# A ring of weight slots in a one-core MoE kernel: twelve slots with a four-slot stash, or sixteen slots in two halves

## What is computed

```python
def expert_choice_moe(h, w_router, w1, w3, w2):
    aff = jax.nn.softmax(jnp.einsum('bsd,de->bse', h, w_router).astype(jnp.float32), axis=-1)
    cap = CAPACITY_FACTOR * S // N_EXPERTS          # 32 tokens for each expert
    gate, idx = lax.top_k(aff.swapaxes(1, 2), cap)
    xe = jax.vmap(lambda hb, ib: hb[ib])(h, idx)

    def expert(args):
        xt, w1e, w3e, w2e = args
        return (jax.nn.silu(xt @ w1e) * (xt @ w3e)) @ w2e
```

## Time and profile before

| | us |
|---|---|
| median of 3 executions | 1844.26 (1843.57 to 1846.16) |
| the profiled execution, timed | 1841.69 |
| its span, first to last instruction | 1839.8 |
| first matmul with expert weights | 595.0 |
| last slot of the last expert arrives | 1830.51 |

### The profile page before, as it was taken

The page is one execution under the profiler, slowest core; times in us unless marked ns, Lnnn a source line. Parts: engine busy times, 40 slices in busy tenths (PEclk is TensorE's granted clock), DMA queues, the critical chain, the costliest instruction groups (busy, mean ns, idle before and its releaser), DMA issues.

```text
span 1839.8 us, 24014 instructions
## 1 busy us (share of the span) xinstructions
PE 1345.1 (73%) x10570; PEld 825.3 (45%) x10570; DVE 272.9 (15%) x555; ACT 226.6 (12%) x531; POOL 42.3 (2%) x68
## 2 busy tenths in 40 slices
PE   6998999999987676666665765666575665757565
PEld 4577888888565234232331423233142332414232
DVE  1215100006952000000010000101000010100001
ACT  1333221012133010010000001000000100000010
POOL 0001000002020000000000000000000000000000
PEclk9999999999998887777777777777777777777777
DMA  9746354242445999999999999999999999999998
GB/s 353 298 160 251 143 224 169 106 183 68 186 189 220 421 436 424 431 434 436 435 427 437 425 429 433 439 428 434 432 430 427 435 437 425 438 428 435 430 432 343
DMA packets 48248, 649.02 MB, mean 353 GB/s; under 512 B 3832, under 2 KB 6336, under 8 KB 31056
## 3 DMA queue, kind: packets, MB, share of 16 engines
q1 hardware_dynamic: 45152, 643.90, 82.9%
q10 hardware_dynamic: 2848, 3.55, 0.6%
q0 software_dynamic: 208, 1.00, 0.1%
HBM read 647.38 MB, written 1.06 MB: 352 GB/s over the span
## 4 chain that ended last, share of the span: by engine, by line
DMA 59%; PE 11%; DVE 1%; issue 1%; ACT 0%; SPq 0%; DVEq 0%; PEldq 0%; ACTq 0%
DMA ring<-in_w 59%; PE ps L1220 11%; DVE arena L1099 0%; DVE small L1103 0%; ACT arena L683 0%; DVE arena L1168 0%; DVE arena L1128 0%; DVE arena L1170 0%; DVE xT L1212 0%; ACT L708 0%; DVE arena L1187 0%; ACT arena L690 0%; SPq L369 0%; DVE arena L1078 0%; ACT arena L711 0%
## 5 line engine op out<-in xcount | busy, mean ns | idle before, releaser
L1220 PE MATMUL ps<-ring,table 128*32 128x352 f32 x4032 | 435.9, 602 | 270.3 <-DMA ring<-in_w 270.2
L1220 PEld LDWEIGHTS ps<-ring,table 128*32 128x32 f32 x4032 | 154.3, 140 | 536.8 <-issue 339.9
L1220 PE MATMUL ps<-ring,arena 128*32 128x256 f32 (+1 forms) x2818 | 197.0, 437 | 150.0 <-DMA ring<-in_w 149.8
L1220 PEld LDWEIGHTS ps<-ring,arena 128*32 128x32 f32 (+1 forms) x2818 | 102.7, 125 | 246.5 <-issue 149.1
L1220 PE MATMUL ps<-hT,ring 128*128 128x256 f32 (+1 forms) x880 | 194.7, 382 | 3.0 <-PE ps L1220 1.4
L1220 PEld LDWEIGHTS ps<-hT,ring 128*128 128x128 f32 (+1 forms) x880 | 165.0, 189 | 30.9 <-issue 6.2
L1220 PE MATMUL ps<-arena,ring 128*128 128x256 f32 (+1 forms) x800 | 175.2, 379 | 1.9 <-ACT arena L632 1.4
L1220 PEld LDWEIGHTS ps<-arena,ring 128*128 128x128 f32 x800 | 151.4, 190 | 23.3 <-issue 2.9
L1220 PE MATMUL ps<-arena 32*128 32x256 f32 (+10 forms) x532 | 91.5, 383 | 29.2 <-DVE xT L1212 12.2
L1220 PEld LDWEIGHTS ps<-arena,hT 128*128 128x128 f32 x512 | 104.1, 315 | 9.1 <-issue 9.1
L1220 PE MATMUL ps<-arena,hT 128*128 (+1 forms) x512 | 106.3, 387 | 1.8 <-DVEq L1196 1.8
(11 more groups left out here) (225 smaller groups left out, 540.5 us busy)
## 6 DMA issues: line engine op xcount, KB each, us to landing
ring<-in_w SPq DMA_DIRECT2D x76, 5632.0 KB, 32.9
ring<-in_w SPq DMA_DIRECT2D x19, 2816.0 KB, 28.3
ring<-in_w SPq DMA_DIRECT2D x35, 1408.0 KB, 31.2
ring<-in_w_ff SPq DMA_DIRECT2D x8, 4096.0 KB, 13.9
ring<-in_w_ada SPq DMA_DIRECT2D x6, 4096.0 KB, 15.2
ring<-in_w_in SPq DMA_DIRECT2D x3, 4096.0 KB, 13.9
ring<-in_w_in SPq DMA_DIRECT2D x5, 2048.0 KB, 19.2
ring<-in_w_out SPq DMA_DIRECT2D x2, 4096.0 KB, 12.8
```

The costliest lines, as they stand in the source:

```text
L1220: return pe.matmul(o, w, x, start=first, stop=last)
```

## The change

`ring` and `arena` become one tensor, `big`, and the ring now has 16 places; places 12 to 15 are where `stash` lay. Since 24 is not a multiple of 16, slot q of expert e lies at place (q + 8 * odd) % 16, where odd is 1 for odd experts. Two experts in turn therefore need different addresses, and the loops of PE and SP now have a body of two experts: PE's loop runs 7 times over experts (1, 2), (3, 4) to (13, 14), and expert 15 is written out once behind it, as expert 0 is ahead of it. The loops of ScalarE, VectorE and GpSimd stay as they were.

Experts 1 to 14 are loaded in six transfers of four slots. Expert 0's w2 is loaded in 1, 1, 2, 4 slots (`FIRST_W2`), right behind its other slots and ahead of expert 1; expert 15's w2 in 4, 2, 1, 1 (`LAST_W2`), as before. There are 133 transfers of expert weights before and 103 after: 11 for expert 0 in both, then 10 + 14 x 8 before and 14 x 6 + 8 after. SP waits for slots 16 back, not 12.

```diff
-NSLOT = 12
+UNIT_SLOTS = 12
+NSLOT = 16
-PIECES = (4, 4, 4, 4, 4, 2, 1, 1)
+FIRST_W2 = (1, 1, 2, 4)
+LAST_W2 = (4, 2, 1, 1)
...
-        ring = sb("ring", NSLOT * SLOT)
-        arena = sb("arena", AR)
+        big = sb("big", UNIT_SLOTS * SLOT + AR)
+        ring = big[:, 0:NSLOT * SLOT]
+        arena = big[:, UNIT_SLOTS * SLOT:]
...
-            for q, n, done in ((0, 1, s["lead_in"]), (1, 1, s["lead_in"]), (2, 2, piece_in[0])):
-                sp.wait_ge(s["w_used"], q + n)
-                slots(1, q, n, done)
...
-            with sp.Fori(0, NE - 2) as e:
-                for i, (q, n) in enumerate(PIECE_AT):
-                    sp.wait_ge(s["w_used"], NCHUNK * e + q + n + 2 * NCHUNK - NSLOT)
-                    piece(e + 2, i)
+            slots(0, 15, 1, piece_in[3])
+            q = 2 * C
+            for i, n in enumerate(FIRST_W2):
+                sp.wait_ge(s["w_used"], q + n - NSLOT)
+                slots(0, q, n, piece_in[4 + i // 3])
+                q += n
+
+            def pieces(e, odd, count=6):
+                for i in range(count):
+                    sp.wait_ge(s["w_used"], NCHUNK * e + 4 * (i + 1) - NSLOT)
+                    slots(e, 4 * i, 4, piece_in[i], odd)
+
+            with sp.Fori(1, NE - 1, 2) as e:
+                pieces(e, 1)
+                pieces(e + 1, 0)
+            pieces(NE - 1, 1, 4)
+            q = 2 * C
+            for i, n in enumerate(LAST_W2):
+                sp.wait_ge(s["w_used"], NCHUNK * (NE - 1) + q + n - NSLOT)
+                slots(NE - 1, q, n, piece_in[4] if i == 0 else last_in[i - 1], 1)
+                q += n
...
-            expert(0, first=True)
-            with pe.Fori(1, NE) as e:
-                expert(e)
+            expert(0, 0, first=True)
+            with pe.Fori(1, NE - 1, 2) as e:
+                expert(e, 1)
+                expert(e + 1, 0)
+            expert(NE - 1, 1, last=True)
```

More of the change, by code:

```diff
@@ L59 @@
 NVEC = sum(n for _, n in VEC.values())
-PIECE_AT = [(sum(PIECES[:i]), n) for i, n in enumerate(PIECES)]
-PIECE_OF = {q: i for i, (q, n) in enumerate(PIECE_AT)}
-assert sum(PIECES) == NCHUNK and all(q % C + n <= C and q % NSLOT + n <= NSLOT for q, n in PIECE_AT)
 def bank_plan():
@@ L247, in build @@
         halfgb = small[:, 88:96]
-        stash = ar(0, 4 * SLOT)
         yacc = xT_[:, :].rearrange("p (st n) -> p st n", st=ST)
@@ L272, in build @@
         unit_in2 = sem("unit_in_gate_columns")
-        piece_in = [sem(f"piece_in{i}") for i in range(len(PIECES))]
+        piece_in = [sem(f"piece_in{i}") for i in range(6)]
+        last_in = [sem(f"last_in{i}") for i in range(3)]
         s = {name: sem(name) for name in """
@@ L280, in build @@
             sq1_set n1_set t1_set h_set relu_set x1_set sq2_set n3_set n2_set up_set sgb_set pe_link
-            qsq_set qk_set rs16_set v_set    csq_set diag_set cvar_set x2_set sq3_set first_in stash_in lead_in sqp_set
+            qsq_set qk_set rs16_set v_set    csq_set diag_set cvar_set x2_set sq3_set first_in stash_in sqp_set
             lge_set wr2_set std_set rst_set lgs_set hnat_set yinit_set xe_set ye_set xe_full sc_full pgT_set hid_full he_set sg_set
@@ L365, in _, with slots @@
                     T["w2_2"].rearrange("e (p r) n -> p e (r n)", r=FR)]
-            def slots(e, q, n, done):
-                at, mat = q % NSLOT, q // C
+            def slots(e, q, n, done, odd=0):
+                at, mat = (q + 8 * odd) % NSLOT, q // C
                 sp.dma_start(ring[:, at * SLOT:(at + n) * SLOT],
                              mats[mat][:, e, (q - C * mat) * SLOT:(q - C * mat + n) * SLOT]).then_inc(done, 16)
-            def piece(e, i):
-                slots(e, *PIECE_AT[i], piece_in[i])
             sp.wait_ge(s["unit_used"], UNIT["qk"] + 1)
@@ L380, in _ @@
             sp.wait_ge(s["xr_set"], 1)
-            piece(0, 0)
+            slots(0, 0, 4, piece_in[0])
             slots(0, 4, 2, s["first_in"])
@@ L385, in _ @@
             slots(0, 8, 1, piece_in[2])
-            stashed = mats[1][:, 0, (12 - C) * SLOT:]
-            sp.dma_start(stash[:, 0:3 * SLOT], stashed[:, 0:3 * SLOT]).then_inc(s["stash_in"], 16)
+            slots(0, 12, 3, s["stash_in"])
             sp.wait_ge(s["std_set"], 1)
-            sp.dma_start(stash[:, 3 * SLOT:], stashed[:, 3 * SLOT:]).then_inc(piece_in[3], 16)
-            for q, n, done in ((0, 1, s["lead_in"]), (1, 1, s["lead_in"]), (2, 2, piece_in[0])):
-                sp.wait_ge(s["w_used"], q + n)
-                slots(1, q, n, done)
-            for i, (q, n) in enumerate(PIECE_AT):
[L394 to L400, removed]
-            with sp.Fori(0, NE - 2) as e:
-                for i, (q, n) in enumerate(PIECE_AT):
-                    sp.wait_ge(s["w_used"], NCHUNK * e + q + n + 2 * NCHUNK - NSLOT)
-                    piece(e + 2, i)
+            slots(0, 15, 1, piece_in[3])
[17 more added lines that the diff above has]
+                q += n
         @block.gpsimd
@@ L1756, in _, with expert @@
             pe.sem_inc(s["sc_full"], 1)
-            def expert(e, first=False):
+            FIRST_AT = ((0, piece_in[0], 1), (4, s["first_in"], 2), (6, piece_in[1], 1), (8, piece_in[2], 1),
+                        (12, s["stash_in"], 1), (15, piece_in[3], 1))
+            def expert(e, odd, first=False, last=False):
                 def gather(g):
@@ L1772, in expert @@
                         q = mat * C + c
-                        slot = q % NSLOT
+                        slot = (q + 8 * odd) % NSLOT
                         if mat == 0:
                             pe.wait_ge(s["xe_set"], C * e + c + 2)
-                        if q in PIECE_OF:
-                            pe.wait_ge(piece_in[PIECE_OF[q]], 16 * (e + 1))
-                        w = ring[:, slot * SLOT:(slot + 1) * SLOT]
[L1779 to L1785, removed]
+                        if first:
+                            for at, done, n in FIRST_AT:
+                                if q == at:
+                                    pe.wait_ge(done, 16 * n)
+                        elif c % 4 == 0:
+                            pe.wait_ge(piece_in[2 * mat + c // 4], 16 * e + 16)
+                        w = ring[:, slot * SLOT:(slot + 1) * SLOT]
                         for half in range(2):
@@ L1802, in expert @@
                 pe.wait_ge(s["pgT_set"], e + 1)
-                w2v = ring[:, 4 * SLOT:12 * SLOT].rearrange("p (r n) -> p r n", r=FR)
+                w2v = ring[:, 8 * odd * SLOT:8 * (odd + 1) * SLOT].rearrange("p (r n) -> p r n", r=FR)
+                steps = FIRST_W2 if first else LAST_W2 if last else (C,)
+                starts = [sum(steps[:i]) for i in range(len(steps))]
                 got = 0
@@ L1806, in expert @@
                     while got * SLOT < (r + 1) * D:
-                        q = 2 * C + got
-                        if q in PIECE_OF:
-                            pe.wait_ge(piece_in[PIECE_OF[q]], 16 * (e + 1))
+                        if got in starts and first:
+                            pe.wait_ge(piece_in[4 + starts.index(got) // 3], 48 if got < 4 else 16)
+                        elif got == 0:
+                            pe.wait_ge(piece_in[4], 16 * e + 48)
+                        elif got in starts and last:
+                            pe.wait_ge(last_in[starts.index(got) - 1], 16)
+                        elif got == 4 and not first:
+                            pe.wait_ge(piece_in[5], 16 * e + 16)
                         got += 1
```

## The result

| | before | after |
|---|---|---|
| median, us | 1843.91 (6 runs) | 1854.43 (6 runs) |
| lowest to highest | 1839.51 to 1848.21 | 1850.16 to 1857.81 |
| profiled execution, span | 1839.8 | 1848.3 |
| first matmul with expert weights | 595.00 | 592.52 |
| last slot of the last expert arrives | 1830.51 | 1839.05 |

The changed kernel is slower: the ratio is 1.0056, 95% interval 1.0041 to 1.0071, and 1854.43 us lies outside the stated range of 1841.0 to 1850.5. The two profiled executions differ by 8.5 us of span only, since the stages ahead of the experts, whose work the change leaves alone, happened to end 2.5 us earlier in the one of after. The stretch from the first expert matmul to the last slot's arrival leaves that out: 11.0 us longer.

What follows compares the result with a forecast made beforehand. The prediction took the DMA stream of expert weights as the bound. Span: 1839.8 - 2.2 (larger transfers) + 6.0 (code fetches) = 1843.6 us; median: 1844.26 + 3.8 = 1848.0 us, range 1841.0 to 1850.5.

Steps and rivals of the forecast that it cites:

- The bound, the start and the end: Expert-weight DMA bounds the kernel; the stream's start changes by zero, and 9.3 us behind the last slot stay.
- The gain from larger transfers: Weight loading: removing w2's cut into 2, 1, 1 and expert 1's 1, 1, 2 gains 15 x 0.15 = 2.2 us.
- PE's later end: PE ends each expert 4.8 us later, waiting for w2's whole second half; covered by the weight stream, costing nothing.
- the wait at w1's second half stays: Sign in PE's loop: the wait of w1's second half is still a wait for DMA.
- The code comes again: PE's two-expert loop body isn't kept, so each branch back refetches it: 62 fetches more, about 90 packets, 6.0 us.
- the price of a fetch: PE code fetches in the weight stream: 0.07 to 0.11 us each, 4.2 to 6.8 us for 62; 6.0 taken.
- The rival of one engine carrying all: Code fetches on a single DMA engine delay every piece 1.1 us each, 68 us, about 1910; 0.05 with PE starving.
- slower: Whole kernel: slower by over 0.2%, from 1847.95 us; chance 0.42, 0.37 from the forecast and 0.05 from a rival.
- the mechanism: The main forecast, PE's loop code fetched again on each branch back, 1848.0 us; chance 0.60.
- A pair of experts was to take about 160.9 us: Sign in the loop: with code fetches, pairs of experts take about 160.9 us; an expert without fetches 79.97.

Runs made afterwards that it cites:

- the experiment on the code alone: Kernel before with only PE's loop changed to a body of two experts, expert 15 written out behind it: 1855.75 us, ratio 1.0059.
- transfers alone: Kernel before, PE untouched, with the cut of w2's second half removed in experts 1 to 14: 1841.58 us, ratio 0.9996.
- after, body of 5.8 blocks: Changed kernel, second halves of w1 and w3 left out for both experts in PE's loop, output not the reference's: 1842.83 us, ratio 0.9989.
- 6.3 and 6.8: Changed kernel, w3's second half left out for both experts in the loop (6.8), also w1's for the first (6.3): 1851.78 us (6.3), 1854.03 us (6.8).
- 7.3 and 7.8: 7.3: changed kernel, w3's second half left out for each pair's first expert in the loop, 1858.93 us; 7.8: changed kernel's full body, 1854.43 us.
- 83 packets: Kernel before with PE's experts 1 to 15 written out, no loop or branch: 1850.84 us, ratio 1.0038.

## Why the prediction was wrong

**The bound, the start and the end** held: DMA share 1.00 in the loop, back at 0.98 between 598 and 600 us, the tail 9.25 us.

**The gain from larger transfers**, 2.2 us, held: 79.98 us for an expert instead of 80.12, and 2.5 us of the stream in the experiment that has nothing else. The time of the whole kernel was too scattered to show it.

**PE's later end** is covered, as said. That the wait at w1's second half stays was right within the loop's body (1.18 us at 1218.42) and wrong behind the branch, where PE needs until w3 to catch up.

**The code comes again**: the mechanism was right. Its count was near: 98 packets against the "about 90" foretold, 68 more against 62, since each turn fetches ten blocks and not nine.

**The step that failed is the price of a fetch.** I bounded the term by 4.2 us for 62 (1.1 us of one engine, spread over 16) and 6.8 us (0.11 for each of expert 1's four fetches) and took 6.0, 0.10 for each. It is 0.20 us each, 13.4 us for 68 in the experiment on the code alone. Of the 7.4 us over my term the six fetches more than foretold are 1.2 us, the higher price is the rest. With 13.4 the sum reads 1843.9 - 2.2 + 13.4 = 1855.1, beside 1854.43 measured.

Both bounds were wrong for reasons that the packet records of the traces show. There each transfer ends with one packet of 4 bytes on each of the 16 engines, so that one can see how far every engine lags behind the first. The records don't name the engine, so the lags below are only sorted. For one transfer late in the stream of three kernels, the lag of the 16 engines behind the first of them, in us:

```
transfers alone (30 packets), at 1734 us:
0 0.07 0.10 0.11 0.13 0.31 0.31 0.34 0.37 1.49 1.50 1.53 1.57 1.65 1.73 1.87
after, body of 5.8 blocks (36 packets), at 1763 us:
0 0.14 0.30 0.34 0.41 0.46 0.61 0.80 1.70 1.97 1.99 2.01 2.13 2.19 2.38 3.60
after (98 packets), at 1596 us:
0 0.15 0.18 0.18 0.24 0.29 0.31 0.93 10.96 11.14 11.72 12.29 12.36 12.41 12.60 12.63
```

In every row at least eight lags stay under 1 us. In the changed kernel the eight small lags are the same from turn to turn, while the mean of the other eight is 2.14 us at 783.33, 4.08 at 943.24, 6.01 at 1103.18, and so on to 11.81 at 1582.94: 1.93 us more in each turn of ten fetches. So eight engines take all the code, in turn. A fetch sets its engine back by about 1.5 us, more than the 1.1 us that its own packet is shown with, since the packet of weights behind it is shown with 2.08 to 2.22 us instead of 1.67, once for each of the 72 fetches between 600 and 1800 us. And a piece has arrived when its last engine is done: 1.5 us / 8 = 0.19 us for each fetch, once they have gone round. The other eight engines, which gained nothing by being early, run out of work at the end: in the 23 us before the last slot's arrival the DMA share is 0.60, where it was 0.91 in the kernel before.

Expert 1's four fetches looked cheap for a reason that the same records show. At 639.30 in the kernel before, three engines were already 1.71 to 1.84 us late from earlier fetches; at 706.06 seven were, by 1.65 to 2.32. The four fetches had set four other engines back to where three already stood, so the latest moved by only 0.48 us. One must not divide the delay of a few fetches by their number when they take turns. The rival of one engine carrying all was at 68 us; half of the engines carrying all is the truth, and I had no case between one and 16.

**The chances.** 0.42 stood on slower, 0.60 on the mechanism. A pair of experts was to take about 160.9 us and took 161.8. The range ended at 1850.5 because it took 0.11 us as the most that a fetch could cost. The packet times in hand (1.1 us on one engine, and nothing that said how many engines take part) allowed anything from 0.07 to 1.1.

**The limit of the loop.** The Trainium skill (Runtime: NRT & Kernel Launch, Instruction fetch mechanics) gives PE's store as 2048 instructions, 8 blocks. Here 5.8 blocks of body were kept and 6.3 were not. If the body begins late in a block, 5.8 blocks touch 7, 6.3 and 6.8 touch 8, and 7.3 and 7.8 touch 9. Two things speak for that. The fetches in a turn are nine for 6.3 and 6.8 blocks and ten for 7.3 and 7.8, one more than the blocks touched. And behind the branch PE stands a second time after 14 matmul records of the gather, as it would if the next block began there. Then 7 blocks are kept and the eighth is in use for the block that comes next. That reading fits the five bodies of two experts; no run here moved the loop's start within its block, so it stays a reading. The same section lets a taken branch fetch its target already when that lies outside a window of two blocks; by that the old body of 3.8 blocks would have come again in each turn, and the earlier trace rows shows no such packet. On the block's size of 256 instructions the trace agrees: 36 and 83 packets came out as counted ahead.

## What to carry to other kernels

When the DMA engines are the bound, an engine's code is traffic too: count the instructions of a loop's body before unrolling it by two, and look at the queue of kind "instruction" in a window of later passes, where a body that is kept shows no packet. A fetch cost 0.20 us here, somewhat more than one expert gained by its larger transfer (0.15). And a cost that lands on some engines in turn must be priced on the engine that is latest, divided by the number that take turns, and that number has to be read from the packets, not assumed.

The larger ring brought nothing here, where the share was already 1.00. Of this change only the larger transfers may be worth keeping, with PE's loop as it was (1841.58 us, not told apart from before by the comparison, 2.5 us shorter in the stream of one profiled execution).

## What the runs showed of the hardware that I had not expected

By the lags, PE's code arrives over 8 of the 16 DMA engines, and each packet of 16 KB holds up its engine by about 1.5 us, while the packet itself is recorded with 1.0 to 1.1. The 16 engines don't share the delay: each carries its own part of every transfer, and the lag of the late ones grew from 2.1 to 11.8 us over five turns of the loop while the others kept their pace.

A loop of 5.8 blocks of 256 instructions is kept and one of 6.3 is not. Once it isn't, all of it comes again in each turn, ten blocks for a body of 7.8, not only the part that exceeds the store: the packets jump from 36 to 90 for half a block more.

Behind the branch back PE stood for 5.3 and 2.8 us before its next instructions were there (5.2 to 6.1 and 2.1 to 3.8 in the other turns), and in code without branches for some 2 us at times. Why eight engines, and which, no run here shows.
